# Square-root steps of four columns, PSUM banks counted over neighbouring places, and a row sum moved behind the next place's matmuls, in a decoder layer with expert retrieval

## The reference

```python
mod = silu(c) @ w_ada + b_ada                 # sh1, sc1, g1, sh2, sc2, g2
h = rmsnorm(x, norm1) * (1 + sc1) + sh1
u, xb, yb, gate_logits = split(h @ w_in)      # 1024, 1024, 1024, 2048 columns
pooled = trailing_mean(u, windows 2, 4, 8, 16) - u
y_a = (pooled @ pool_mix * pool_scale) @ w_branch_a
xc = causal_conv4(xb)
r, i = sigmoid(xc @ w_rg + b_rg), sigmoid(xc @ w_ig + b_ig)
log_a = -8 * r * softplus(-lru_lambda)
hs = scan(h = exp(log_a) * h + sqrt(1 - exp(2 * log_a)) * i * xc)
y_b = (hs * gelu(yb)) @ w_branch_b
x = x + g1 * ((sigmoid(gate_a) * y_a + sigmoid(gate_b) * y_b) @ w_out)
h = rmsnorm(x, norm2) * (1 + sc2) + sh2
# expert retrieval, 8 heads, 2 x 128 keys, the 16 best pairs of each head
idx, gsm = top16(h @ w_q, sub_keys)           # 128 experts for each token
wts = gsm * gelu(h . expert_u[idx])
x = x + g2 * sum(wts * expert_v[idx]);  y = rmsnorm(x, final_norm)
```

## Time and profile before

| | |
|---|---|
| median of three runs | 2020.98 us |
| the profiled execution | 2021.08 us, span 2019.3 us |
| TensorE busy | 1701.4 us (84%) |
| VectorE busy | 1336.1 us (66%) |
| ScalarE busy | 1062.3 us (53%) |
| GpSimd busy | 780.8 us (39%) |
| moved by DMA | 730.12 MB, mean 362 GB/s |
| chain that ended last | PE 39%, DMA 33%, DVE 17%, ACT 8%, issue 3% |

### The profile page before, as it was taken

The page is one execution under the profiler, slowest core; times in us unless marked ns, Lnnn a source line. Parts: engine busy times, 40 slices in busy tenths (PEclk is TensorE's granted clock), DMA queues, the critical chain, the costliest instruction groups (busy, mean ns, idle before and its releaser), DMA issues.

```text
span 2019.3 us, 17203 instructions
## 1 busy us (share of the span) xinstructions
PE 1701.4 (84%) x5376; PEld 897.0 (44%) x5376; DVE 1336.1 (66%) x2966; ACT 1062.3 (53%) x2068; POOL 780.8 (39%) x591
## 2 busy tenths in 40 slices
PE   6999969898899999968899877787877778777776
PEld 3899965354445555534444332332232233332222
DVE  3460346999878688888666667676666677666554
ACT  2251036433585332334466666766667567676765
POOL 1000012343323344444344444555545445454563
PEclk9899989899899999989899999999999999899999
DMA  9856259899778899999999999999999999999996
GB/s 393 357 206 219 91 219 370 328 383 368 291 304 338 327 380 403 378 377 370 355 368 398 406 403 414 413 400 406 410 409 416 416 409 412 394 410 407 413 421 278
DMA packets 105020, 730.12 MB, mean 362 GB/s; under 512 B 13200, under 2 KB 13728, under 8 KB 17248
## 3 DMA queue, kind: packets, MB, share of 16 engines
q0 software_dynamic: 83104, 604.05, 74.3%
q1 hardware_dynamic: 20160, 122.12, 15.8%
q10 hardware_dynamic: 1664, 2.85, 0.4%
HBM read 725.91 MB, written 3.06 MB: 361 GB/s over the span
## 4 chain that ended last, share of the span: by engine, by line
PE 39%; DMA 33%; DVE 17%; ACT 8%; issue 3%; POOL 1%; SPq 0%; DVEq 0%; ACTq 0%; POOLq 0%
DMA t_uv_rows<-in_expert_uv,t_arena 23%; PE bank L662 19%; PE v_sum L746 8%; DMA t_uv_rows<-in_expert_uv,t_idx 8%; PE v_sum L747 8%; DVE t_uv_rows L1335 6%; ACT t_uv_rows L917 4%; DVE t_uv_rows L1346 3%; DMA t_uv_rows<-in_w_in 1%; ACT t_wts L911 1%; DMA t_uv_rows<-in_w_ada 1%; POOL t_uv_rows L571 1%; PE bank L675 1%; ACT t_gelus L909 1%; DVE t_choice L1241 1%
## 5 line engine op out<-in xcount | busy, mean ns | idle before, releaser
L746 PE MATMUL v_sum<-t_uv_rows,t_ident 128*128 128x512 f32 (+1 forms) x940 | 530.6, 647 | 263.5 <-ACT t_uv_rows L917 213.1
L571 POOL DMA_INDIRECT t_uv_rows<-in_expert_uv,t_arena x384 | 505.4, 1316 | 500.4 <-PE v_sum L747 481.4
L1335 DVE CUSTOM_DVE_ANT_0 t_uv_rows<-t_uv_rows,t_arena 128x1024 f32<-128x1024 f32 x384 | 469.0, 1226 | 342.8 <-DMA t_uv_rows<-in_expert_uv,t_arena 337.8
L917 ACT ACTIVATE t_uv_rows<-t_uv_rows,t_wts 128x1024 f32<-128x1024 f32 x470 | 539.7, 1148 | 15.3
L571 POOL DMA_INDIRECT t_uv_rows<-in_expert_uv,t_idx x192 | 266.6, 1389 | 711.7 <-DVEq L1320 278.9
L662 PE MATMUL bank<-t_arena,t_weights 128*128 128x384 f32 (+1 forms) x1824 | 522.0, 444 | 9.9 <-issue 7.1
L747 PE MATMUL v_sum<-t_uv_rows,t_ident 128*128 128x512 f32 (+1 forms) x940 | 500.8, 615 | 0.0
L909 ACT ACTIVATE t_gelus<-t_dots 128x1 f32<-128x1 f32 x576 | 114.6, 199 | 626.1 <-DVE t_dots L1335 625.1
L662 PEld LDWEIGHTS bank<-t_arena,t_weights 128*128 128x128 f32 x1824 | 334.6, 193 | 204.4 <-issue 52.4
L746 PEld LDWEIGHTS v_sum<-t_uv_rows,t_ident 128*128 128x128 f32 (+1 forms) x940 | 157.2, 192 | 571.1 <-ACT t_uv_rows L917 431.7
L747 PEld LDWEIGHTS v_sum<-t_uv_rows,t_ident 128*128 128x128 f32 (+1 forms) x940 | 181.8, 193 | 243.4 <-issue 243.4
(11 more groups left out here) (201 smaller groups left out, 1005.9 us busy)
## 6 DMA issues: line engine op xcount, KB each, us to landing
t_weights<-in_w_in SPq DMA_DIRECT2D x26, 1024.0 KB, 9.0
t_weights<-in_w_q SPq DMA_DIRECT2D x16, 1024.0 KB, 7.4
t_uv_rows<-in_w_in SPq DMA_DIRECT2D x14, 1024.0 KB, 12.2
t_uv_rows<-in_w_ada SPq DMA_DIRECT2D x13, 1024.0 KB, 19.9
t_weights<-in_w_ada SPq DMA_DIRECT2D x11, 1024.0 KB, 10.6
...
t_uv_rows<-in_expert_uv,t_arena POOLq DMA_INDIRECT x384, 9.6
...
```

Of the source, the lines that this page charges most:

```text
L571: pool.indirect_dma_start(out=row(r), out_offset=None, in_=A["expert_uv"], in_offset=bass.IndirectOffsetOnAxis(ap=idx_of(t)[:, n:n + 1], a ...
L746: nc.tensor.matmul(v_sum[0:m, 0:512], add, v[:, 0:512], start=first, stop=last)
L917: nc.scalar.activation(v, v, ACT.Copy, scale=wts[:, col(r)]).then_inc(scaled_done, 1)
L1335: V.tensor_tensor_reduce(out=u, in0=u, in1=h2_rows(t), scale=1.0, scalar=0.0, op0=ALU.mult, op1=ALU.add, accum_out=dots[:, col(r)]).then_i ...
```

## The change

**Rates.** `rates` handles four columns at a time instead of two, in ScalarE's order four Tanh, four Exp, two square roots; there are two steps to a group instead of four. The scan steps of group 1 keep their steps of two columns.

**Banks.** `pack` puts a unit into a place only if the products of that place and of either neighbour are at most six together (`crowded`). The units of group 1 from `rgig` 1 on come to lie in other places, most of them one place later. Place 32, for one, now has no unit, place 33 `rgig` 1, place 34 the first `rates` step and `yb` 2 and 3, place 35 `lru` 0 and `rgig` 2, place 36 no unit of TensorE, place 37 `rgig` 3, `u` 6 and `lru` 1, place 38 the second `rates` step and `u` 7. `mix` goes in two halves around `mg` 8.

**Sums.** For a closing pair VectorE's adds stay in their place (role `add`), but TensorE's sum of the fourth row comes after the units of the following place.

**The start.** Ten `ada` parts stand ahead of the first column product instead of 14; the other ten follow one to four units instead of six, one to three, and the second `modT` comes after the last of them.

**The final step.** The products of g2 and of the final norm are made in stages 1 and 2 instead of 0 and 2, and for tile 0 the stages 1 to 3 lie at places 58 to 60 instead of 32 to 34.

```diff
+def lagged(p):
+    return mode(p) == "close"
...
     if kind == "final":
-        return [(("g2", "fn")[b // 2], g, i) for i in range(2)] if b in (0, 2) else []
+        return [(("g2", "fn")[b - 1], g, i) for i in range(2)] if b in (1, 2) else []
...
-        for q in range(4):
-            units += [("rates", g, q)] + [("yb", g, c) for c in range(2 + 2 * q, 4 + 2 * q) if c < 8] + [("lru", g, q)]
+        for r in range(2):
+            units += [("rates", g, r)] + [("yb", g, c) for c in ((2, 3, 4), (5, 6, 7))[r]] + [("lru", g, 2 * r), ("lru", g, 2 * r + 1)]
...
-        units += [("mix", g, q) for q in range(4)]
-    units += [("mg", g, c) for c in range(8, 16)]
+        units += [("mix", g, 0), ("mix", g, 1), ("mg", g, 8), ("mix", g, 2), ("mix", g, 3)]
+    units += [("mg", g, c) for c in range(8 if g == 0 else 9, 16)]
...
+def crowded(places, n, unit):
+    def banks(units):
+        return sum(len(products_of(u)) for u in units)
+    here = banks(places[n]) + banks([unit])
+    return max(here + banks(places[n - 1]), here + banks(places[n + 1])) > NBANK
...
-            banks = sum(len(products_of(u)) for u in places[n] + [unit])
-            if n >= earliest and fits and banks <= NBANK:
+            if n >= earliest and fits and not crowded(places, n, unit):
...
-    start = ada[:4] + [[("square", 0, 0)]] + ada[4:6] + [[norm]] + ada[6:8] + [[scale[0]], [("modT", 0, 0)]] + ada[8:10] + [[scale[1]], [scale[2]]] + ada[10:12] + [[scale[3]]] + ada[12:14]
-    later = ada[14:20]
+    start = ada[:4] + [[("square", 0, 0)]] + ada[4:6] + [[norm]] + ada[6:8] + [[scale[0]], [("modT", 0, 0)]] + ada[8:9] + [[scale[1]], [scale[2]]] + ada[9:10] + [[scale[3]]]
+    later = ada[10:20]
     for n, unit in enumerate(mixer_units(0)):
         start.append([unit])
-        if n % 3 == 2 and later:
+        if n % 4 == 3 and later:
             start.append(later.pop(0))
...
         if after:
-            return [("sum", "pair", t, j)] + [("both", "final", t, 0)] * (j == PAIRS_OF[t] - 1)
-        return [("pair", "pair", t, j)] + [("both", "final", t - 1, j + 1)] * (t > 0 and j < 3)
+            own = [("add", "pair", t, j)] + [("sum", "pair", t, j)] * (not lagged(n))
+            behind = [("sum", "pair") + pairs[n - 1]] * (n > 0 and lagged(n - 1))
+            return behind + own + [("both", "final", t, 0)] * (j == PAIRS_OF[t] - 1)
+        late = 26 if t == 1 else 0
+        return [("pair", "pair", t, j)] + [("both", "final", t - 1, j - late + 1)] * (t > 0 and late <= j < late + 3)
...
-            def rates(g, q):
+            def rates(g, half):
                 r, root = cols("conv", g), cols("gb", g)
-                act.wait_ge(taken["rgig"], nth(("rgig", g, 4 * q + 3)))
-                for c in (2 * q, 2 * q + 1):
+                four = range(4 * half, 4 * half + 4)
+                act.wait_ge(taken["rgig"], nth(("rgig", g, 8 * half + 7)))
+                for c in four:
                     nc.scalar.activation(root[:, c, :], r[:, c, :], ACT.Tanh, scale=sp2[:, c:c + 1], bias=sp2[:, c:c + 1])
-                for c in (2 * q, 2 * q + 1):
+                for c in four:
                     nc.scalar.activation(r[:, c, :], r[:, c, :], ACT.Exp, scale=minus_sp4[:, c:c + 1], bias=minus_sp4[:, c:c + 1]).then_inc(rates_done, 1)
-                act.wait_ge(rates_done, 2 * (4 * g + q + 1))
-                two = root[:, 2 * q:2 * q + 2, :]
-                nc.scalar.activation(two, two, ACT.Sqrt, scale=0.25).then_inc(sqrt_done, 1)
+                act.wait_ge(rates_done, 4 * (2 * g + half + 1))
+                for q in (2 * half, 2 * half + 1):
+                    two = root[:, 2 * q:2 * q + 2, :]
+                    nc.scalar.activation(two, two, ACT.Sqrt, scale=0.25).then_inc(sqrt_done, 1)
```

More of the change, by code:

```diff
@@ L127, in mixer_units @@
         units += [("conv", g, c) for c in range(6, 8)]
[L128 to L130 removed]
+        units += [("rgig", g, 0), ("rgig", g, 1), ("rates", g, 0), ("yb", g, 2), ("yb", g, 3), ("lru", g, 0), ("rgig", g, 2), ("rgig", g, 3),
+                  ("u", g, 6), ("lru", g, 1), ("rates", g, 1), ("u", g, 7), ("mg", g, 0), ("lru", g, 2), ("mg", g, 1), ("mg", g, 2), ("lru", g, 3), ("mg", g, 3)]
         for q in range(4):
             units += [("mg", g, 4 + q), ("pool", g, q)]
[L133 to L134 removed]
+        units += [("mix", g, 0), ("mix", g, 1), ("mg", g, 8), ("mix", g, 2), ("mix", g, 3)]
+    units += [("mg", g, c) for c in range(8 if g == 0 else 9, 16)]
     units += [(k, g, c) for k in ("ba", "bb") for c in range(8)]
@@ L161, in before @@
     kind, g, b = unit
-    return {"conv": [(("xb", g, b), 1)], "rgig": [(("conv", g, 2 * b + 1), 2)], "rates": [(("rgig", g, b), 1)],
-            "lru": [(("rates", g, b), 1), (("yb", g, 2 * b + 1), 1)], "mg": [(("lru", g, b // 2) if b < 8 else ("pool", g, 3), 1)],
+    return {"conv": [(("xb", g, b), 1)], "rgig": [(("conv", g, 2 * b + 1), 2)], "rates": [(("rgig", g, 2 * b + 1), 1)],
+            "lru": [(("rates", g, b // 2), 1), (("yb", g, 2 * b + 1), 1)], "mg": [(("lru", g, b // 2) if b < 8 else ("pool", g, 3), 1)],
             "pool": [(("lru", g, 3), 1)], "mix": [(("pool", g, 3), 1)],
@@ L754, in _ @@
                         pe.wait_ge(norm_in, 16)
-                        of = 2 if b else int(g > 0)
+                        of = 2 if b == 2 else int(g > 0)
                         half = slice(product[2] * 512, (product[2] + 1) * 512)
@@ L942, in _ @@
                             scale_row(2 * p + i)
-                elif role in ("make", "sum"):
+                elif role in ("make", "add", "sum"):
                     continue
@@ L1375, in _ @@
                     dot(g, 2 * b + 1)
-                elif role == "sum":
+                elif role == "add":
                     p = PAIR0[g] + b
@@ L1381, in _ @@
                         add_on(2 * p)
-                elif role == "make":
+                elif role in ("make", "sum"):
                     continue
@@ L1396, in _ @@
                 elif kind == "rates":
-                    rates(g, b)
+                    rates(g, 2 * b)
+                    rates(g, 2 * b + 1)
                 elif kind == "lru":
```

5 lines of the change are left out of this document (1 added, 4 removed).

## The result

| kernel | median | runs |
|---|---|---|
| before | 2019.04 us (2013.18 to 2028.12) | 7 |
| changed | 2029.60 us (2026.57 to 2036.74) | 7 |

The ratio is 1.0051 (95% interval 1.003 to 1.0072): slower by half a per cent, where I forecast 0.8% faster, and outside my range (1994 to 2014). The profiled execution took 2033.17 us, against 2021.08 before.

A forecast was written before the change was run, and what follows sets the result against it. TensorE was taken to bound the gain in places 32 to 50, and full DMAs tiles 2 to 4. Banks, start, final step and sums gave 2021.1 − 18 + 1.7 + 2 − 3 = 2004 us, range 1994 to 2014, chance 0.50.

The forecast's parts named there:

- Sums behind the next unit: From 694 to 925 us, TensorE's next unit no longer held while VectorE adds: −3 us, between 0 and −6.9.
- (c): Rival: closing pairs' fourth row freed 3.1 us later, places 49 to 87; 2069 us, or 2028 for a third; chance 0.14.
- Banks kept apart: Places 32 to 50: TensorE's waits for banks ScalarE has not read fall away; −18 us, between 0 and 27 saved.
- in the stretch with TensorE at 204.4 of 231, which has room: 694 to 925 us: column unit mg 11, 5.4 us, moves here from 528 to 694 and finds room.
- the 14.1 us of idle as a bound: 528 to 694 us: TensorE's idle time, 166 − 151.9, one part of the 27.1 us at most for the banks.
- By itself worth 0: Rates in two steps: group 1 saves 7.8 us of ScalarE, which has 66 us free there, so no gain alone.
- the one of 3.83 us: 528 to 694 us: one of two TensorE waits before gate units whose banks ScalarE had not read; the other 4.41.
- The block itself: A four-column rates step on ScalarE: 10.7 us, with TensorE idle 5 to 8 us beside the first.
- GpSimd's wait for sums from 31 to 50: Sign, places 31 to 50: GpSimd's 102.4 us wait for TensorE's sums before gathering new rows goes down by half.
- The start: Four w_ada blocks after the first w_in block; first column product about 42, second turn waits about 3: +1.7 us.
- The final step of tile 0: Moved from places 32 to 34 to 58 to 60, where VectorE is at 83% and DMAs full: +2 us, between 0 and 4.

The follow-up runs named there:

- before_lag: The kernel before with one edit, each closing pair's fourth-row sum behind the following place's units: ratio 1.0142 to before.
- no_lag_start0: The changed kernel with all closing pairs' sums in front of the next place's units and the old start put back: ratio 0.9986 to before.
- rates_only: no_lag_start0 with the old bank rule, keeping the rates in two steps, the final step at 58 to 60 and mix in halves: ratio 0.9949 to before.
- rates_final0: rates_only with the final step of tile 0 back at places 32 to 34: ratio 0.9974 to before.
- no_lag: The changed kernel with every closing pair's sum in front of the next place's units again, all else kept: 2022.93 us, ratio 0.9988 to before.
- banks_only: The kernel before with the new bank rule alone: ratio 0.9952 to before.
- both_early: no_lag_start0 with mg 9 to 11 laid at places 48 to 50 and the rest packed from 51 on: ratio 0.9938 to before.

## Why the prediction was wrong

Sum by the profiles, against 2021.1: 9 to 95 without the late sums −7.7; the start +4.3; the late sums +17.4. That is 2035.1, and the execution took 2033.2. By the ratios the late sums cost some 13 us, and all the rest together gave 2.4. Against the forecast the late sums are 20.4 us of the miss and the banks 10.3.

- **Sums behind the next unit: −3 forecast, +17.4 measured. This is the step that failed.** I counted the 23.2 us that TensorE waits for adds as what could come out, and took the row's longer stay as a rival. The mechanism is (c)'s, the slot of the fourth row, but not its price or its spread: 3.1 us for each of 20 pairs was wrong, since the price is not that of a unit's 5.4 us. Behind place 50 most sums cost next to nothing, and the whole lies at two spots, 6 us at place 71 and 7 at 83 and 85. What counts is a unit ahead of the sum that itself waits, because it is the first to need a result of another engine (7.28, 7.11 us; 17.43 in before_lag). Then the gather behind it waits 5 to 15 us longer than with the sum in front. That the total of (c) "for a third" (2028) came near was chance.
- **Banks kept apart: −18 forecast; −17.7 measured in its stretch, −7.7 kept. This step failed as well.** The match in the stretch is luck: the rates, `mix` and the final step gave part of it, and some 13 of the 17.7 us are busy time of TensorE that left the stretch, not idle time. What was kept is less sure than the 7.7: by its ratio (0.9986) no_lag_start0 kept some 3 us. That the column unit that leaves the stretch is done later "in the stretch with TensorE at 204.4 of 231, which has room" was wrong. Work that the dots leave behind is done in 50 to 95, where added work costs about two thirds of its time. Of the 6 to 9 us that the seven variants with prompt sums above won from 9 to 95, 2 to 6 are TensorE's time without work (69 us before, 628.3 less 145.4, 152.1 and 261.5; 63 to 67 there). The rest is busy time, 554 to 558 us instead of 559, for as many records (1607 before, 1605 to 1609 there). I had the 14.1 us of idle as a bound and should have taken it less the work that only moves.
- **"By itself worth 0" for the rates** missed a wait, worth some 4 us: in the kernel before ScalarE read the third gates at 575.79 us, behind its second step of rates (from 565.21) and two rows' weights, and TensorE's fourth stood 4.41 us for that the earlier trace rows. In rates_only the third and the fourth are made and read without a wait, ahead of the second block; TensorE, then ScalarE:

```profile
561.59 2.74 PE L689 MATMUL bank<-t_arena,t_weights 128*128 128x384 f32 x8
...
565.88 2.74 PE L689 MATMUL bank<-t_arena,t_weights 128*128 128x384 f32 x8
```

```profile
565.11 1.98 ACT L874 ACTIVATE t_arena<-bank,t_vecs 128x384 f32<-128x384 f32 x4
...
570.63 1.98 ACT L874 ACTIVATE t_arena<-bank,t_vecs 128x384 f32<-128x384 f32 x4
...
580.05 2.49 ACT L882 ACTIVATE t_arena<-t_arena,t_sp 128x384 f32<-128x384 f32 x4
```

In rates_final0 that 4.41 us wait is 0.66, too, while the one of 3.83 us stays. So the longer step cures one of the two waits that I gave to the bank rule. The block itself was sized right: in the changed kernel 10.49 us (565.43 to 575.92) against 10.7, with TensorE standing 4.95 us behind it (5 to 8 named); ScalarE, then TensorE:

```profile
565.43 2.49 ACT L882 ACTIVATE t_arena<-t_arena,t_sp 128x384 f32<-128x384 f32 x4
...
574.63 1.28 ACT L851 ACT_TABLE_LOAD   x1
575.92 0.87 ACT L851 ACTIVATE t_arena<-bank 128x384 f32<-128x384 f32 x2
```

```profile
580.73 2.07 PE L760 MATMUL v_sum<-t_uv_rows,t_ident 128*128 128x512 f32 x2 [4.95 <-DVE t_uv_rows L1362]
```

- **GpSimd's wait for sums from 31 to 50** fell from 102.4 to 78.0 us, not by half.
- **The start: +1.7 forecast, +4.3 measured.** The first column product came at 42.25 (42 named), the second turn waited 3.80 us for VectorE (3). Not counted: that turn behind its wait took 10.25 us for its 48 records, 8.58 before.

```profile
42.25 5.44 PE L676 MATMUL bank<-t_arena,t_weights 128*128 128x192 f32 x32 [1.67 <-ACT t_arena L827]
...
115.27 10.25 PE L642 MATMUL bank<-t_fold,t_arena 128*128 128x9 f32 x48 [3.80 <-DVE t_arena L1050]
```

- **The final step of tile 0: +2 forecast, not confirmed.** From 9 to 95 the move gave 0.3 and 2.2 us (no_lag and rates_only against their twins with it at 32 to 34), by the ratios 0.2% in both pairs, with overlapping intervals. I had priced its VectorE work behind place 50 and not the banks that it held at places 32 to 34.

rates_only (0.9949), banks_only (0.9952) and both_early (0.9938) beat both kernels, by 0.5 to 0.6% against before and 1.0 to 1.1% against the changed one (ratio of ratios). Open stays why the seven orders with prompt sums all end at 620 to 622 us from 9 to 95 in their profiles, while their ratios go from 0.9938 to 1.001 (the new start is 0.2% of that), and what part of TensorE's 41 to 46 us without work from 50 to 95 could be had.
